# A hybrid attention/SSD layer on one core: attention heads spread over 5/4 chunks, gating in quarters, x turned in pairs

## What is computed

```
h   = RMSNorm(x)
u   = h @ W_in            -> q, k, v (16 heads of 64), forget logits, xs, B, C, z, dt
y_A = forgetting attention over 16 heads, causal
y_B = RMSNorm(SSD(silu(conv4(xs, B, C)), dt) * silu(z))      16 heads, chunked scan
x   = x + concat(y_A, y_B) @ W_out
x   = x + W_down(silu(conv3(RMSNorm(x) W_gate)) * (RMSNorm(x) W_up))
x   = x + sigmoid(RMSNorm(x) W_pg) * (p @ W_pp)
out = RMSNorm(x)
```

## Time and profile before

| | |
|---|---|
| median of three runs | 1228.5 us |
| profiled execution, its own time | 1229.56 us |
| its span (first to last instruction) | 1227.8 us |
| mean granted clock of TensorE | 0.998 |
| TensorE busy | 1214.0 us, 99% |
| TensorE weight loads | 1044.3 us, 85% |
| VectorE busy | 817.8 us, 67% |
| ScalarE busy | 644.7 us, 53% |
| GpSimd busy | 49.0 us, 4% |
| data moved | 231.67 MB, mean 189 GB/s |

### The profile page before, as it was taken

The page is one execution under the profiler, slowest core; times in us unless marked ns, Lnnn a source line. Parts: engine busy times, 40 slices in busy tenths (PEclk is TensorE's granted clock), DMA queues, the critical chain, the costliest instruction groups (busy, mean ns, idle before and its releaser), DMA issues.

```text
span 1227.8 us, 18711 instructions
## 1 busy us (share of the span) xinstructions
PE 1214.0 (99%) x6522; PEld 1044.3 (85%) x6522; DVE 817.8 (67%) x1130; ACT 644.7 (53%) x879; POOL 49.0 (4%) x69
## 2 busy tenths in 40 slices
PE   9999999999999999999999999999999999999997
PEld 8888888888788888888888888888888888888885
DVE  4798787888766667677676776776745454545554
ACT  6565787675555444454444454544434443435554
POOL 3200220002200000000000000000000000000000
PEclk9999999999999999999999999999999999999999
DMA  8666875445655666656666666666666656566662
GB/s 263 183 181 182 240 242 177 124 135 184 200 180 176 188 192 191 191 183 193 194 184 192 188 188 188 188 190 188 191 199 188 191 189 193 185 196 219 197 192 103
DMA packets 184616, 231.67 MB, mean 189 GB/s; under 512 B 11104, under 2 KB 135604, under 8 KB 184436
## 3 DMA queue, kind: packets, MB, share of 16 engines
q1 hardware_dynamic: 182708, 225.92, 59.7%
q0 software_dynamic: 1824, 5.04, 1.4%
q10 hardware_dynamic: 32, 0.01, 0.0%
HBM read 227.22 MB, written 2.14 MB: 187 GB/s over the span
## 4 chain that ended last, share of the span: by engine, by line
PE 95%; DVE 2%; ACT 1%; POOL 1%; DMA 1%; issue 0%; SPq 0%; POOLq 0%; ACTq 0%; DVEq 0%
PE ps L382 35%; PE ps L380 18%; PE ps L1023 7%; PE ps L1022 7%; PE ps L1024 6%; PE ps L414 6%; PE ps L416 6%; PE ps L415 6%; PE ps L354 1%; DVE w_lo L343 1%; PE ps L823 1%; DMA w_raw<-in_w_in 1%; PE ps L921 1%; PE ps L936 0%; ACT w_hi L338 0%
## 5 line engine op out<-in xcount | busy, mean ns | idle before, releaser
L343 DVE TENSOR_TENSOR w_lo<-w_raw,w_hi 128x1024 fp32r<-128x1024 f32 x412 | 507.0, 1235 | 325.4 <-ACT w_hi L338 324.5
L382 PE MATMUL ps<-h_parts,w_hi 128*128 128x512 f32 x1920 | 668.7, 392 | 0.0
L338 ACT ACTIVATE w_hi<-w_raw 128x1024 fp32r<-128x1024 f32 x412 | 435.1, 1059 | 439.2 <-PE ps L382 248.3
L380 PE MATMUL ps<-h_parts,w_lo 128*128 128x256 f32 x1920 | 540.3, 281 | 0.8 <-DVE w_lo L343 0.8
L382 PEld LDWEIGHTS ps<-h_parts,w_hi 128*128 128x128 f32 x1920 | 359.3, 187 | 78.9
L380 PEld LDWEIGHTS ps<-h_parts,w_lo 128*128 128x128 f32 x1920 | 362.8, 189 | 1.4 <-issue 1.0
L1022 PE MATMUL ps<-w_hi,act_parts 128*128 128x512 f32 x352 | 137.2, 390 | 0.0
L1024 PE MATMUL ps<-w_hi,act_parts 128*128 128x512 f32 x352 | 137.0, 389 | 0.0
L1023 PE MATMUL ps<-w_lo,act_parts 128*128 128x512 f32 x352 | 137.0, 389 | 0.0
L1024 PEld LDWEIGHTS ps<-w_hi,act_parts 128*128 128x128 f32 x352 | 66.1, 188 | 13.8
L1022 PEld LDWEIGHTS ps<-w_hi,act_parts 128*128 128x128 f32 x352 | 66.1, 188 | 13.7
(11 more groups left out here) (254 smaller groups left out, 927.2 us busy)
## 6 DMA issues: line engine op xcount, KB each, us to landing
w_raw<-in_w_gate_up SPq DMA_DIRECT2D x352, 256.0 KB, 3.2
w_raw<-in_w_down SPq DMA_DIRECT2D x88, 512.0 KB, 4.6
w_raw<-in_w_in SPq DMA_DIRECT2D x87, 512.0 KB, 3.8
w_raw<-in_w_out SPq DMA_DIRECT2D x32, 512.0 KB, 4.7
w_raw<-in_w_ple_gate SPq DMA_DIRECT2D x32, 512.0 KB, 4.6
ssd_spread<-ssd_rows_dram POOLq DMA_DIRECT2D x16, 192.0 KB, 4.3
w_raw<-in_w_ple_proj SPq DMA_DIRECT2D x4, 512.0 KB, 5.2
out_x<-xtok SPq DMA_DIRECT2D x8, 256.0 KB, 2.9
```

The source lines that it names most:

```text
L338: act.activation(parts(n)[0], w_raw[:, n % RING, :], ACT.Copy).then_inc(w_hi_made, 1)
L343: dve.tensor_tensor(lo, w_raw[:, n % RING, :], hi, ALU.subtract).then_inc(w_lo_made, 1)
L380: pe.matmul(ps[:, bank_of[m], T:2 * T], lo, both[:, 0, :], start=first and k == 0, stop=False, skip_group_check=True)
L382: mm = pe.matmul(ps[:, bank_of[m], :], hi, both.rearrange("p b t -> p (b t)"), start=False, stop=last and k == tiles // len(bank_of) - 1, ...
```

## The change

- Attention step i stands behind chunk a0 + 5i/4 (rounded down) in place of a0 + i, a0 = 63: chunks 63 to 85, every fifth one free of a head. split_fox(b) follows behind 86 + b in place of 82 + b (89 + b on ScalarE and VectorE).
- leave_z(b) stands at the earliest behind chunk 88 on ScalarE: 0 to 2 at 88, 3 at 90 (before: 82, 82, 86, 90). gate_mul is cut from two halves to four quarters, one chunk behind each: 89, 89, 89, 91 on VectorE (before: 83, 91). GpSimd squares each quarter when it is gated.
- In q0, x is loaded as pieces of 1, 1, 2, 2, 2 pairs of tiles in place of 1, 1, 1, 1, 2, 2. Chunks 1, 2 and 3 turn two pairs each, one behind the second pass and one behind the chunk: pairs 2 and 3, 4 and 5, 6 and 7. Chunks 4 to 6 turn none.
- ScalarE makes h tiles 2n and 2n+1 ahead of w_hi of chunk n; before, behind it.

```diff
@@ X_PIECES, multiply_by_pass @@
-    X_PIECES = [(a, a + 1) for a in range(RING)] + [(a, a + 2) for a in range(RING, KD // 2, 2)]
+    X_PIECES = [(0, 1), (1, 2)] + [(a, a + 2) for a in range(2, KD // 2, 2)]
...
             one_pass(w_hi, 0)
-            if turn is not None and turn_behind == 1:
-                turn()
             pe.wait_ge(h_lo_made, top_k + 1)
             one_pass(w_hi, 1)
-            if turn is not None and turn_behind == 2:
+            if turn is not None:
                 turn()
@@ plan @@
             a0 = end["v0"]
+            fox_at = lambda i: a0 + i * 5 // 4
             for i in range(H + 3):
-                after(pe_after, a0 + i, "fox", i)
-                after(act_after, a0 + i + LEAD, "fox", i)
-                after(dve_after, a0 + i + LEAD - 1, "fox", i)
+                after(pe_after, fox_at(i), "fox", i)
+                after(act_after, fox_at(i) + LEAD, "fox", i)
+                after(dve_after, fox_at(i) + LEAD - 1, "fox", i)
             for b in range(WT // 2):
-                all_after(a0 + H + 3 + b, "split_fox", b)
+                all_after(fox_at(H + 2) + 1 + b, "split_fox", b)
             for half in range(2):
                 for b in range(2):
-                    after(act_after, max(end[f"z{half}{'ab'[b]}"], a0 + H) + LEAD, "leave_z", 2 * half + b)
-                after(dve_after, end[f"z{half}"] + LEAD + 1, "gate_mul", half)
+                    n = max(end[f"z{half}{'ab'[b]}"], fox_at(H + 2)) + LEAD
+                    after(act_after, n, "leave_z", 2 * half + b)
+                    after(dve_after, n + 1, "gate_mul", 2 * half + b)
@@ GpSimd @@
-                pool.wait_ge(gated, b // 2 + 1)
+                pool.wait_ge(gated, b + 1)
@@ multiply_q0 @@
+                early = (None, 2, 4, 6)[c] if c < 4 else None
                 multiply_by_pass(pe, c, tiles, g.banks, (w_hi_made, c + 1), (w_lo_made, c + 1),
-                                 (lambda: turn_x(c + 1)) if c + 1 < NORM else None).then_inc(w_used, 1)
+                                 early and (lambda: turn_x(early))).then_inc(w_used, 1)
+                if early:
+                    turn_x(early + 1)
@@ ScalarE @@
+            act.wait_ge(gain_copied, 1)
             for n in range(len(front)):
+                if n < NORM:
+                    for k in (2 * n, 2 * n + 1):
+                        make_h(0, k, par_mix)
                 if n == 0:
...
-                    for k in range(2):
-                        make_h(0, k, par_mix)
...
-                if 0 < n < NORM:
-                    for k in (2 * n, 2 * n + 1):
-                        make_h(0, k, par_mix)
@@ VectorE @@
-            def gate_mul(half):
+            def gate_mul(b):
...
-                dve.wait_ge(z_made, 2 * half + 2)
-                tiles = slice(MT * half, MT * (half + 1))
+                dve.wait_ge(z_made, b + 1)
+                tiles = slice(2 * b, 2 * b + 2)
```

More of the change, by code:

```diff
@@ L347, in chunk_of, with multiply_by_pass @@
             return g.view[:, k * c:k * c + k, g.col:g.col + g.cols]
-        def multiply_by_pass(pe, n, tiles, bank_of, hi_made, lo_made, turn=None, turn_behind=1):
+        def multiply_by_pass(pe, n, tiles, bank_of, hi_made, lo_made, turn=None):
             def one_pass(parts_, part):
@@ L776, in multiply_q0 @@
                 if c == 0:
-                    multiply_by_pass(pe, 0, tiles[:MT], g.banks, (first_hi_made, 1), (first_lo_made, 1), lambda: turn_x(1), 2)
+                    multiply_by_pass(pe, 0, tiles[:MT], g.banks, (first_hi_made, 1), (first_lo_made, 1), lambda: turn_x(1))
                     multiply_by_pass(pe, 0, tiles[MT:], g.banks, (w_hi_made, 1), (w_lo_made, 1)).then_inc(w_used, 1)
                     return
+                early = (None, 2, 4, 6)[c] if c < 4 else None
                 multiply_by_pass(pe, c, tiles, g.banks, (w_hi_made, c + 1), (w_lo_made, c + 1),
-                                 (lambda: turn_x(c + 1)) if c + 1 < NORM else None).then_inc(w_used, 1)
+                                 early and (lambda: turn_x(early))).then_inc(w_used, 1)
+                if early:
+                    turn_x(early + 1)
             def turn_par():
@@ L1237, in _ @@
                     copy(w_hi[:, 0, 0:COLS], w_raw[:, 0, 0:COLS]).then_inc(first_hi_made, 1)
-                    act.wait_ge(gain_copied, 1)
-                    for k in range(2):
-                        make_h(0, k, par_mix)
                     act.wait_ge(w_landed[0], 16)
```

## The result

The changed kernel takes 1234.5 us (median of 5 runs, 1233.65 to 1235.06), the kernel before 1228.5 us: ratio 1.0045, 95% interval 1.0034 to 1.0055. The profiled execution took 1234.6 us by its own time, its span is 1232.9 us, 5.1 us longer than before. Between the medians lie 6.0 us, since the profiled execution of the kernel before was itself 1.1 us above its median.

A forecast was written before the change was run, and what follows sets the result against it. TensorE, busy 99% of the span, was taken as the bound, its four waits, some 3.4 us, as the ceiling of gain. Terms -0.86 - 0.78 + 6.6 - 0.79 = +4.2 us gave a median of 1232.7 us, range 1229.3 to 1235.3.

The forecast's parts named there:

- The first new wait: In front of chunk 88: TensorE waits 1.0 us for the first mixLo piece, done 6.4 us after chunk 86's start.
- the second: In front of chunk 89: TensorE waits 5.1 us for mixLo(1), behind gate_muls and steps alternating with GpSimd's squares.
- the first projection: Chunks 0 to 8: chunk 1 starts at 11.1, not 11.72; chunk 8 at 34.66, not 35.52: -0.86 us, bounds -1.5 and 0.
- the waits behind the heads: New waits in front of chunks 88 to 91 for the four mixLo pieces: 1.0, 5.1, 0.1 and 0.4, sum +6.6 us.
- the old waits: Waits at L901 (last attention head's values) and L959 (gated norm's sum) both go: -0.78 and -0.79 us.
- rival A: The clock falls too, after TensorE idles 5.1 us: 2.0 us more, bounds 1.0 and 2.7, time 1234.7; chance 0.26.
- the prediction's own sign: Wrong if mixLo(1) lands before chunk 88 ends, or if the clock row shows 0.5 inside the span.
- main line: Whole kernel: the summed terms give +4.2 us, median 1232.7, with no clock fall; chance 0.47 together with rival D.
- the sentence against it: Against the clock's fall: the stretch without work is hardly longer than the one that shows a fall.
- the two small waits behind it: In front of chunks 90 and 91, for mixLo(2) and mixLo(3): 0.1 and 0.4 us.
- The wait in front of chunk 2: x tiles turned one pass later, so h and w_hi come later: chunk 2 starts at 15.65 in place of 15.10.
- the sum without it: Sum of +4.2 us, without the Trainium skill's 1.38 us drain per table switch; with it, 1.4 us higher.

The follow-up runs named there:

- the filler run: The changed kernel with 40 transposes of the identity into an unused bank on TensorE in front of the wait at chunk 89: 1232.94 us, 1.0036.
- leave_z back: The changed kernel with leave_z on ScalarE where it was, behind chunks 82, 82, 86, 90, everything else as changed: 1233.59 us, 1.0038.
- The split runs: The kernel before with one half of the change each: new first projection alone 1228.48 us, 0.9996; new heads, split and gating alone 1234.9 us, 1.0054.

## Why the prediction was right, and where not

**Direction, place and mechanism.** The forecast was 1232.7 us, the measurement 1234.5. The first new wait was put at 1.0 us and measured 0.8 to 0.9, the second at 5.1 and measured 4.9 to 5.0. The walk along the lists of VectorE and ScalarE, counted from chunk 86's start (289.31), had the two mixLo pieces at 6.4 and 14.25 and they came at 6.4 and 14.1.

**The sum came out nearer than its terms.** In the span the forecast was +4.2 us and the profiles show +5.1. The clock, which the sum left out, added 1.46, and the first projection gained 0.7 less than forecast; against that the waits behind the heads came to 5.85 in place of 6.6, 0.5 went in small changes that nobody forecast, and 0.1 more came from the old waits. That these nearly cancel is luck. The other 0.9 us between the medians is the slow profiled execution of the kernel before, no event in these two traces.

**The clock was the wrong side of a choice.** I gave the half clock 0.26 and priced it at 1.0 to 2.7 us, with 2.0 taken (rival A, 1234.7). It came: 1.46 us in the profiled execution, and 1234.7 is the nearer of the two forecasts. By the prediction's own sign, 0.50 in the clock row inside the span, its main line is wrong, for this one term, which it held at nothing. The mean granted clock of the five runs is 0.994 to 0.997; the kernels without a fall have 0.997 or 0.998, so the mean shows it in some runs and can't in the others. The step that failed is the sentence against it, that the wait is hardly longer than the stretch that shows a fall; that was no reason against a fall. It also hid the two small waits behind it, 0.5 us in my sum, which the filler run brought back (0.55).

**The first projection, predicted -0.86, measured -0.16.** From chunk 1 to chunk 8 the account held: 23.56 us predicted, 23.58 measured in the changed kernel, 23.80 in the kernel before. What failed is the start of chunk 1, predicted 11.1, measured 11.77. That start moves by itself: with the old first projection it is 11.72, 10.88 and 11.23 in three profiles, with the new one between 10.58 and 11.90 in eight. In the changed kernel's profile the first matmuls ran at half rate until about 9.4, before at most until 7.6, and so x was turned at 9.9 in place of 9.1. With the new projection it follows the moment from which the full clock is granted: 10.58 to 10.79 where that is at 5.3 to 6.6 us, 11.32 where it is at 8.4, 11.75 to 11.90 at 9.4 to 9.65. Chunk 0 may add to it, with its w_hi behind h now: it starts at 7.04 to 7.34 in the eight and at 6.73 to 6.94 in the three, where the prediction put 0 to 0.3. A single profile can't place a gain of 0.6 us there, and the run of this part alone leaves it open (1228.48 against 1228.74).

The wait in front of chunk 2 is as forecast: chunk 1 was to last 4.55 us, from 11.1 to 15.65, and lasts 4.48. In the run with its turn behind the first pass it lasts 3.77, so the late turn cost 0.7. In the changed kernel:

```profile
13.78 0.60 PE L764 MATMUL ps<-ident,xtok 128*128 128x128 f32 x4
...
16.25 2.18 PE L354 MATMUL ps<-h_parts,w_hi 128*128 128x256 f32 x16 [0.48 <-ACT w_hi L338]
```

**The old waits.** L901 and L959 went, 0.78 and 0.89. That the second goes without the spread heads is shown by the version with the old heads and gate_mul in quarters, where chunk 93 takes 2.96 us with the gated norm's matmuls in place of 3.86.

**Table load.** ScalarE's Silu starts 0.01 us behind the end of its table load (289.91 + 1.28, 291.20), so the drain of about 1.38 us in the Trainium skill (ScalarE: Activation LUTs, What ACT_TABLE_LOAD costs) is again not there, and the sum without it is the one that held.

**Not settled:** 0.5 us of the changed kernel's lead at chunk 86 comes from small differences between chunks 8 and 86. The split runs show 0.2 of it with the first projection alone and 0.3 with heads and gating alone; what they are, no run takes apart.

## What to carry to other kernels

Where each engine works through its own fixed list, price a moved step by walking the lists from the last common point, and count what stands in front of the step that TensorE waits for, not only the step itself: here split_fox could move four chunks later for 0.3 us, and a table load, three Silus and three products in front of it, with what GpSimd and the clock made of them, cost 7 us (1.0045 against 0.9985). A step that starts GpSimd's two-input work belongs behind the urgent VectorE steps, since the two then take turns: here six VectorE steps took 2.87 us more. When the sum gives an idle stretch of TensorE as long as one that lost the clock elsewhere in the trace, put the clock into the sum.

## What was not expected

Half clock behind a long wait can cost less than it seems, since the next steps are late anyway: of 1.46 us, 0.55 would have been waits. And the price moves from run to run: chunk 89, 2.72 us before, takes 4.18 in the changed kernel's profile, 4.45 with leave_z back and 4.94 with heads and gating alone, behind waits of 4.9, 3.8 and 4.9 us. What sets it is how far into the chunk the clock stays at 0.50: until 306.3 us (chunk start 303.49), 305.7 (302.21) and 307.5 (303.02), and half of each overlap, 1.4, 1.7 and 2.2 us, is what the chunk took more. The start is as restless: chunk 1 begins within a range of 1.3 us with the same code of the first projection; the 21 runs of the kernel before in the first session spread over 2.0 us.
